# A two-layer hybrid decoder on one core: cached pages loaded a sequence ahead, begin and RMS norms rebuilt

## What is computed

```python
def rms_norm(x, g):
    y = x * lax.rsqrt(jnp.mean(x * x, axis=-1, keepdims=True) + NORM_EPS)
    return y * g

def run_trunk(x, pos0, mem_kv, nsa_past, gdn_state, p):
    for i in range(DEPTH):
        h = rms_norm(x, p['norm_mix_g'][i])
        if i % N_MIXERS == 0:
            proj = h @ p['nsa_w_in'][li]     # sparse attention over paged key/value rows
            o_mix, rows, win = nsa_layer_mix(...)
        else:
            proj = h @ p['gdn_w_in'][li]     # gated DeltaNet
            o_mix, S, buf = gdn_mix(...)
        o_mem = cross_attend(proj[..., -XA_WIDTH:], mem_kv[i])
        x = x + jnp.concatenate([o_mix, o_mem], axis=-1) @ p['w_out'][i]
        h = rms_norm(x, p['norm_ffn_g'][i])
        x = x + jnp.square(jax.nn.relu(h @ p['w_up'][i])) @ p['w_down'][i]
    y = rms_norm(x, p['final_norm_g'])
```

## Time and profile before

| | |
|---|---|
| median of 3 runs | 1997.31 us (1995.83 to 1998.23) |
| profiled execution | 2001.48 us, its span 1999.7 us |
| TensorE busy | 1893.6 us, 95% |
| VectorE busy | 1049.5 us, 52% |
| ScalarE busy | 520.3 us, 26% |
| GpSimd busy | 39.5 us, 2% |
| transfers | 175.46 MB, mean 88 GB/s |

### The profile page before, as it was taken

The page is one execution under the profiler, slowest core; times in us unless marked ns, Lnnn a source line. Parts: engine busy times, 40 slices in busy tenths (PEclk is TensorE's granted clock), DMA queues, the critical chain, the costliest instruction groups (busy, mean ns, idle before and its releaser), DMA issues.

```text
span 1999.7 us, 26775 instructions
## 1 busy us (share of the span) xinstructions
PE 1893.6 (95%) x10027; PEld 1522.5 (76%) x10027; DVE 1049.5 (52%) x2334; ACT 520.3 (26%) x1294; POOL 39.5 (2%) x48
## 2 busy tenths in 40 slices
PE   7999999998979999999989999899998999999997
PEld 6788555666758888888877787688876888888885
DVE  4441777655565444454446665456555544444444
ACT  2221777233312212100012523333341212210000
POOL 0000000000001000000010000000000000000001
PEclk9999999999989999999999999999998999999998
DMA  6532200566422222222233112100012122222211
GB/s 229 190 129 64 80 1 1 169 195 184 149 106 84 85 85 84 73 78 83 85 121 136 64 64 68 74 1 1 32 41 72 66 85 85 84 85 85 85 64 45
DMA packets 60801, 175.46 MB, mean 88 GB/s; under 512 B 6529, under 2 KB 39442, under 8 KB 47362
## 3 DMA queue, kind: packets, MB, share of 16 engines
q1 hardware_dynamic: 58050, 163.05, 24.4%
q0 software_dynamic: 2624, 10.70, 1.3%
HBM read 160.80 MB, written 12.93 MB: 87 GB/s over the span
## 4 chain that ended last, share of the span: by engine, by line
PE 82%; DVE 6%; SPq 5%; ACT 4%; issue 3%; DMA 1%; POOL 0%; DVEq 0%; POOLq 0%; ACTq 0%
PE psum L1818 58%; PE psum L1341 5%; SPq L492 3%; PE psum L758 2%; PE psum L902 2%; SPq L487 1%; PE psum L739 1%; ACT sbuf L802 1%; PE psum L721 1%; DVE sbuf L1677 1%; PE psum L1796 1%; PE psum L641 1%; PE psum L1899 1%; PE psum L1893 1%; PE psum L1931 1%
## 5 line engine op out<-in xcount | busy, mean ns | idle before, releaser
L1818 PE MATMUL psum<-sbuf 128*128 128x272 f32 x5152 | 1196.1, 393 | 4.5 <-ACT sbuf L2093 1.4
L1818 PEld LDWEIGHTS psum<-sbuf 128*128 128x128 f32 x5152 | 972.7, 190 | 215.6 <-issue 11.3
L1341 PE MATMUL psum<-sbuf 128*128 128x128 f32 (+3 forms) x1020 | 125.8, 279 | 12.4 <-DVE sbuf L1661 5.2
L1341 PEld LDWEIGHTS psum<-sbuf 128*128 128x128 f32 (+3 forms) x1020 | 118.7, 191 | 19.5 <-DVE sbuf L1661 6.0
L2043 ACT ACTIVATE sbuf<-sbuf 128x544 f32<-128x544 f32 x32 | 20.8, 651 | 396.9 <-DVE sbuf L2387 387.5
L902 PE MATMUL psum<-sbuf 128*128 128x256 f32 x448 | 106.7, 389 | 7.1 <-DMA sbuf<-in_pages 7.1
L2266 DVE TENSOR_TENSOR sbuf<-sbuf 128x512 f32<-128x512 f32 x92 | 63.4, 689 | 81.4 <-PE psum L1818 73.6
L902 PEld LDWEIGHTS psum<-sbuf 128*128 128x128 f32 x448 | 82.8, 190 | 24.0 <-DMA sbuf<-in_pages 8.1
L2270 DVE TENSOR_TENSOR sbuf<-sbuf 128x512 f32<-128x512 f32 x92 | 63.8, 693 | 52.2 <-PE psum L1818 50.5
L1520 ACT ACTIVATE sbuf<-psum 128x384 f32<-128x384 f32 (+2 forms) x84 | 40.2, 480 | 106.0 <-PE psum L1341 80.8
L2279 DVE TENSOR_TENSOR sbuf<-sbuf 128x512 f32<-128x512 f32 x92 | 63.1, 686 | 0.0
(11 more groups left out here) (390 smaller groups left out, 2026.9 us busy)
## 6 DMA issues: line engine op xcount, KB each, us to landing
sbuf<-in_w SPq DMA_DIRECT2D x100, 1024.0 KB, 4.9
sbuf<-in_pages SPq DMA_DIRECT2D x256, 128.0 KB, 2.4
sbuf<-in_mcache SPq DMA_DIRECT2D x2, 4096.0 KB, 15.4
sbuf<-in_win SPq DMA_DIRECT2D x8, 512.0 KB, 4.8
out_win_o<-sbuf POOLq DMA_DIRECT2D x8, 512.0 KB, 3.0
sbuf<-in_state SPq DMA_DIRECT2D x6, 512.0 KB, 5.7
out_state_s<-sbuf POOLq DMA_DIRECT2D x6, 512.0 KB, 3.1
sbuf<-in_x SPq DMA_DIRECT2D x1, 2176.0 KB, 11.9
```

The lines of the kernel that those rows point to most:

```text
L1341: last = mm(bank(pair[x])[0:rows, width * (h - h0):width * (h - h0 + 1)], lhs(h), rhs(h), start=True, stop=True)
L1818: ins = mm(to, lhs(k), rhs(k), start=first and k == 0, stop=k == 3, skip_group_check=True)
```

## The change

Three places are changed. First, SP's `sequence` is split into `to_compress(s)` and `to_attend(s)`, each of which calls `places(s)`; pages to compress of sequence s + 1 are issued ahead of pages to attend of sequence s. Second, in the begin TensorE runs three matmuls on constants (`idle_work`), takes the squares of the memory tile by tile, makes the keys and values of layer 0 ahead of x's sums, and x's squares are added up on VectorE (`first_squares`), so that TensorE only spreads one sum (`first_norm_sums`); panel 1 is loaded ahead of x. Third, norms 2 and 4 go by token: the squares are summed into one column for each block of 128 tokens (`token_norm_sums`), root and reciprocal work on 5 columns, and six matmuls spread the factors back over all partitions into PSUM, from which VectorE's products read them. For this the projection of the first tile of layer 1 uses another pair of PSUM banks.

```diff
             panel(0)
+            panel(1)
             sp.dma_start(xT, x_in).then_inc(in_x, 16)
-            for i in range(1, 4):
-                panel(i)
+            panel(2)
+            panel(3)
...
-            def sequence(s):
-
-                at = places(s)
+            def to_compress(s):
                 if s >= 3:
                     sp.wait_ge(w1_used, s - 1)
-                pages(s, at, page_cmp, slice(0, 2 * P), in_cmp)
+                pages(s, places(s), page_cmp, slice(0, 2 * P), in_cmp)
+
+            def to_attend(s):
                 if s == 1:
                     sp.wait_ge(prompt_done, 24)
                 if s >= 2:
                     sp.wait_ge(so_done, s - 1)
-                pages(s, at, page_kv, slice(2 * P, 4 * P), in_pages)
+                pages(s, places(s), page_kv, slice(2 * P, 4 * P), in_pages)
...
+            to_compress(1)
             for s in range(1, NS):
-                sequence(s)
+                if s > 1 and s < NS - 1:
+                    to_compress(s + 1)
+                to_attend(s)
+                if s == 1:
+                    to_compress(2)
...
+            def token_norm_sums(n):
+
+                pe.wait_ge(sq_added, 6 * n)
+                for ci, at in enumerate(BLOCKS):
+                    mm(bank(6)[:, ci:ci + 1], sq_sum[:, at:at + P], ones[:, 0:1], start=True, stop=True)
+                pe.wait_ge(sq_ready, (n + 1) * KT)
+                for ci, at in enumerate(BLOCKS):
+                    last = mm(bank(7)[:, ci:ci + 1], sq[:, 1, at:at + P], ones[:, 0:1], start=True, stop=True)
+                last.then_inc(sq_used, 1)
+                pe.wait_ge(dve_step, RSTD_READY[n])
+                for ci, lo, hi in SPREADS:
+                    half, at = lo // HALF, BLOCKS[ci]
+                    last = mm(both(3)[:, half, lo - HALF * half:hi - HALF * half],
+                              rstd_t[:, ci:ci + 1].to_broadcast([P, P]), ident[:, lo - at:hi - at], start=True, stop=True)
+                last.then_inc(pe_step, 1)
...
             def memory_sums():
                 pe.wait_ge(in_common, 16)
-                pe.wait_ge(mem_sq, KT)
+                idle_work(pe, 5, 3)
                 for k in range(KT):
+                    pe.wait_ge(mem_sq, k + 1)
                     last = mm(bank(0)[:, 0:MEM], ones, sqm[:, k, :], start=k == 0, stop=k == KT - 1)
...
             memory_sums()
-            for k in range(KT):
-                square_sums(k)
-            memory_kv()
+            memory_kv(0)
+            first_norm_sums()
+            memory_kv(1)
...
             def norm(n, gain):
+                if n in RSTD_READY:
+                    dve.wait_ge(sq_used, n + 1)
+                    own(dve.tensor_copy(rms_t, bank(6)[:, 0:5]))
+                    tt(rms_t, rms_t, bank(7)[:, 0:5], ALU.add).then_inc(dve_step, 1)
                 dve.wait_ge(std_ready, n + 1)
-                own(dve.reciprocal(rstd, rstd))
+                if n in RSTD_READY:
+                    dve.reciprocal(rstd_t, rms_t).then_inc(dve_step, 1)
+                    dve.wait_ge(pe_step, RSTD_SPREAD[n])
+                else:
+                    own(dve.reciprocal(rstd, rstd))
...
+            def first_squares():
+                for k in range(1, KT):
+                    dve.wait_ge(sq_ready, k + 1)
+                    if k > 1:
+                        dve.wait_ge(dve_step, k - 1)
+                    tt(rstd, rstd, sq[:, k % 2, :], ALU.add).then_inc(dve_step, 1)
```

More of the change, by code:

```diff
@@ L615, in build, with idle_work @@
         scored = lambda g: 8 * (g // 2) + 1 + max(m for m in range(8) if PAIR[m][0] == g % 2)
+        def idle_work(pe, b, n):
+            for _ in range(n):
+                pe.matmul(bank(b)[:, 0:256], ident, common_ap[:, 0:256], start=True, stop=True)
         def compress_prompt(pe):
@@ L1770, in _, with first_norm_sums @@
             mm = pe.matmul
-            def square_sums(k):
-                pe.wait_ge(sq_ready, k + 1)
+            def first_norm_sums():
+                pe.wait_ge(dve_step, SQUARES_ADDED)
                 for half in range(2):
-                    last = mm(both(3)[:, half, :], ones, halves_of(sq[:, k % 2, :])[:, half, :],
-                              start=k == 0, stop=k == KT - 1)
+                    last = mm(both(3)[:, half, :], ones, halves_of(rstd)[:, half, :], start=True, stop=True)
                 last.then_inc(sq_used, 1)
@@ L1795, in single @@
                     for half in range(2):
-                        last = mm(both(3)[:, half, :], view(ring[slot], KT, 256)[:, k, 0:P], halves_of(hT[:, k, :])[:, half, :],
+                        last = mm(both(3 - l)[:, half, :], view(ring[slot], KT, 256)[:, k, 0:P], halves_of(hT[:, k, :])[:, half, :],
                                   start=k == 0, stop=k == KT - 1)
@@ L1876, in down @@
                                  TSUM[f"down{l}"] + 4 * c)
-                norm_sums(n)
+                token_norm_sums(n)
             def memory_sums():
                 pe.wait_ge(in_common, 16)
-                pe.wait_ge(mem_sq, KT)
+                idle_work(pe, 5, 3)
                 for k in range(KT):
+                    pe.wait_ge(mem_sq, k + 1)
                     last = mm(bank(0)[:, 0:MEM], ones, sqm[:, k, :], start=k == 0, stop=k == KT - 1)
                 last.then_inc(pe_step, 1)
[L1886 to L1891, removed]
-                        for k in range(KT):
[L1893 to L1901, removed]
@@ new lines, in memory_kv @@
+            def memory_kv(l):
+                pe.wait_ge(in_panel[2 * l], 16)
+                wk, wv = view(ring[2 * l], KT, MEM), view(ring[2 * l + 1], KT, MEM)
+                for hp in range(2):
+                    for k in range(KT):
+                        if hp == 0:
+                            pe.wait_ge(memn_ready, KT * l + k + 1)
+                        last = mm(bank(1 + 2 * l)[:, MEM * hp:MEM * (hp + 1)], wk[:, k, P * hp:P * (hp + 1)],
+                                  memn[:, l, k, :], start=k == 0, stop=k == KT - 1)
+                last.then_inc(pe_out, 1)
+                pe.wait_ge(in_panel[2 * l + 1], 16)
+                for m in range(2):
+                    for k in range(KT):
+                        last = mm(bank(2 + 2 * l)[:, MEM * m:MEM * (m + 1)], memn[:, l, k, P * m:P * (m + 1)],
+                                  wv[:, k, :], start=k == 0, stop=k == KT - 1)
+                last.then_inc(pe_out, 1)
@@ L1912, in scores @@
                         if l:
+                            pe.wait_ge(act_out, 2)
                             pe.wait_ge(in_mkv1, 16)
@@ L2034, in first_norm @@
                 for k in range(KT):
[L2035 to L2038, removed]
+                    if k >= 3:
+                        act.wait_ge(dve_step, k - 2)
+                    f(sq[:, k % 2, :] if k else rstd, xT[:, k, :], ACT.Square).then_inc(sq_ready, 1)
             def square(n, k):
@@ L2084, in silu_gates, with inputs_out @@
                 f(c, c, ACT.Silu).then_inc(conv_done, 1)
-            def inputs_out(name, units, tile, pair, after_p1, after_p5, after):
+            def inputs_out(name, l, units, tile, pair, after_p1, after_p5, after):
                 act.wait_ge(pe_out, obase[name] + 1)
-                f(halves_of(tile), both(3), ACT.Copy).then_inc(act_out, 1)
+                f(halves_of(tile), both(3 - l), ACT.Copy).then_inc(act_out, 1)
                 for U in range(ubase[name], ubase[name] + units):
@@ L2139, in memory_norm, with memory_kv @@
                 f(rstdm, bank(0)[:, 0:MEM], ACT.Sqrt, bias=C["eps"], scale=1.0 / D).then_inc(mem_std, 1)
[L2141 to L2146, removed]
+            def memory_kv(l):
+                for half in range(2):
+                    act.wait_ge(pe_out, 2 * l + half + 1)
+                    f((mkv0, mkv1_tmp)[l][:, 512 * half:512 * (half + 1)], bank(1 + 2 * l + half), ACT.Copy)\
+                        .then_inc(memkv_ready, 1)
             def memory_attention(l):
```

35 lines of the change are left out of this document (24 added, 11 removed).

## The result

The changed kernel takes 2048.83 us (median of 4 runs, 2046.17 to 2051.33) against 1997.38 (median of 4): the ratio is 1.0258, with a 95% interval of 1.024 to 1.0276. It is slower by 51.5 us; 51.1 was forecast. Its profiled execution took 2046.67, span 2044.9, so the two traces differ by 45.2 us.

What follows compares the result with a forecast made beforehand. TensorE's back-to-back matmuls were taken to bound the kernel, with SP's queue pacing the sample stage. Terms -7.8 + 61.1 + 2.1 - 3.0 - 1.3 = +51.1 us on 1997.3 gave 2048 us, range 2033 to 2060.

Steps and rivals of the forecast that it cites:

- The bound: Sample stage: SP's queue already sets the pace with almost nothing in hand, so added instructions are paid in full.
- The size of the stage: Sample stage: seven added groups of 16 reads make a sequence 37.3 us instead of 27.6, +61.1 us.
- the clock: Sample stage: TensorE restarts slowly after waits, hidden by SP except after the last one, +2.1 us.
- rival B: Sample stage: reads run near their undisturbed pitch of 0.54 us, stage +43.9, 2031 us in all; chance 0.12.
- The begin: Begin: first projection starts at 43.8 instead of 51.44, -7.8 us, bounds -9.9 and -5.9.
- rival E: Begin gains nothing: a wait for x or its sums replaces the one removed, 2056 us; chance 0.06.
- Norm 2: Norm 2: products start 1.4 us earlier and the matmul group after it takes 7.53 instead of 9.13, -3.0 us.
- Norm 4: Norm 4: products start 1.4 us earlier, with up to 0.05 us more for each of eight reading PSUM, -1.3 us.
- C: Sample stage: the clock stays at 1.2 GHz and TensorE, about 52 us a sequence, becomes the pace, 2122 us; chance 0.03.
- D: Sample stage: the second reading of numbers is hidden and the 7.1 us of waits vanish, -19.2, 1978 us; chance 0.04.

Runs made afterwards that it cites:

- the longer execution above: Profiled execution (1990.38 us) of the changed kernel with numbers read once, sequence 2's pages to compress issued early, norm 2's gaps filled with constant matmuls; median 1987.89 us.

## Why the prediction was right, step by step

**The bound.** SP's in-order queue as the pace of the sample stage, and the seven added groups of reads as the cost: right. Taking the reads out removes the loss whatever the order, and putting them into the old order makes it.

**The size of the stage.** Forecast +61.1 and 2.1 for the clock, together 63.2, measured +55.8. The sum was made with 37.3 us for a sequence, measured 36.4. The reads cost what was taken (9.66; 9.4 to 9.9 seen). The term that was off is the 16 transfers: 8.74 from the crowded mixture of before, 8.22 in the changed kernel (354.37 and 572.21). So rival B was right for the transfers and wrong for the reads. From the first of those transfers to the scores of sequence 6 are 212.1 us instead of the 218.3 of the forecast, and from there to the scores of sequence 7 (594.70) 28.2, where 26.0 and 2.1 were forecast: the slow restart was sized right. Of the 7.4 us too much about 6.2 are the transfers, 0.5 the first group of reads, and 0.8 the value matmuls of the last sequence, which took 2.60 where they had taken 3.44. The waits came where they were said to come, but smaller: 7.1 to 9.1 us for 11 in sequences 3 to 6, 11.2 for 16 in sequence 2, 5.3 for 8 in the compression. With its slow restart TensorE's own part of a period was 27.7 to 29.0 us and not 26.0; SP's queue hides this, so it changed the waits and not the sum.

**The begin.** Forecast -7.8 (its terms as written add up to -7.7), measured -7.2. The memory's sums ended at 10.8 (11.3 taken) and keys and values began at 13.81 (14.05), but the restart behind 2.96 idle us cost 1.8, where 1.0 was taken: the first half of the keys and values took 8.85 for 7.09. The additions on VectorE stood in the shadow, as said. x landed at 16.6 and its sums ended at 25.2, ahead of their use at 29.4, so rival E did not come to pass.

**Norm 2.** Forecast -3.0, measured +1.1; this step failed, in both terms. The spreading matmuls were costed at 1.65 us from a row at full clock, but took 2.77 at 0.50, which left 0.3 of the 1.4. And the projection behind them did not take the 7.53 of an undisturbed one but 10.52: the wait of 5.30 was cut into gaps of 1.0, about as said, but the granted clock was at 0.50 from the spreading on. Kernels with either norm show 9.0 to 10.6, and only fillers brought 7.54 to 7.61, in three kernels.

**Norm 4.** Forecast -1.3, measured -0.8. The spreading took 2.20 for 1.65. The products that read PSUM took 5.62, none of the extra that was allowed for.

**What was not forecast.** Between the first projection and the sample stage the changed kernel's trace is another 2.4 us shorter, with the same instructions, and between norm 2's projection and norm 4 it is 1.3 shorter; the longer execution above shows how the clock makes such differences. The medians are 51.5 apart and the traces 45.2 because the profiled execution of before (2001.48) was long for its kernel and that of after (2046.67) short. That the forecast met the median within a microsecond is thus partly luck: errors of -7.4 in the stage and +4.1 in norm 2 stand against each other. The four parts measured come to +48.9; 3.7 less by what was not forecast and 6.3 more by which executions were profiled give the 51.5.

**The rivals.** B was half right, as told. C did not happen: within each sequence the clock came back, and SP stayed the pace. D would have needed reads of 0.25 us. The Trainium skill (DMA: Bandwidth & Descriptors, Latency and other measured facts) has a floor of about 600 ns for a register load. A group of 16 in sequence took 9.4 to 9.9 us in these traces, 0.6 each, though single undisturbed pairs stood 0.54 apart. The page's figure would have served as well as my mean.

## What to carry to other kernels

Count what an in-order transfer queue executes, not only what it moves: here 16 register reads cost more than the 16 transfers they serve, and a helper that was called in each of two halves doubled them. Loading ahead pays only if the queue has time left in a period; first make the work in the queue smaller than the period of its consumer, then reorder, and use its idle stretches (here 138 us before `prompt_done`) for whatever already has a free buffer. And when a step that the critical engine waits for is made shorter, look at the granted clock behind it: in norm 2 the shortened wait gave 0.3 us and filling it 2.7 in the traces. A filler has to last nearly until the next work can start: behind the one that ended 0.8 us ahead of it (in the begin) the matmuls ran at full speed, behind the one that ended 2.65 us ahead they did not.

## What the runs showed of the hardware

- A register read from the page table and its two register instructions take SP 0.54 us undisturbed and about 0.6 in the mean; a page transfer of 128 KB with its register work 0.51 to 0.57.
- TensorE's granted clock fell to 0.50 (1.2 of 2.4 GHz) for some 12 us while TensorE was busy all the time with matmuls of 66 columns and then wider ones, in one execution and not in another; 64 rows of 66 columns took 11.63 instead of 7.33 us. The Trainium skill (TensorE: Matmul & The Clock Gate, Part 1) describes the low state as one of idling and calls cold matmul counts variable from run to run. Here the low state came in a stretch whose rows show no idling beyond a gap of 0.75 us.
- With matmuls on constants in the gaps of norm 2 the projection after it took 7.54 to 7.61 us in three kernels, instead of 9.0 to 10.6. In two of the three the granted clock still fell to 0.50 for about 3 us in the filled gap and was back at 1.00 for the projection; in the third, the one with more waits filled, it stayed at 1.00.
- Eight products of 544 columns on VectorE took 5.62 us with the factor read from PSUM and 5.66 with it in SBUF.
